# Zero products ahead of the first matmul, squares of the first tiles on POOL, and the first head's groups four dense steps later, in a two-block transformer kernel

## The chip, the cores and the metric

One core of one Trainium2 chip. The metric is the device time of one execution in microseconds (us). The kernel before takes 1307.53 us, the median of three runs (1307.06 to 1307.54).

## The reference

A sequence of 512 tokens with 1024 features passes two blocks. The first is gated DeltaNet (8 heads of 128, in chunks) and an MLP with a squared ReLU; the second has a short convolution, a stick-breaking attention, a spatial gate, an MLP and a gated projection. The change touches only the beginning of the first block:

```python
def rmsnorm(x, g):
    xf = x.astype(jnp.float32)
    y = xf * lax.rsqrt(jnp.mean(xf * xf, axis=-1, keepdims=True) + RMS_EPS)
    return (y * g.astype(jnp.float32)).astype(x.dtype)
...
    proj = h @ w_in
    qkv, gate, a_raw, b_raw = jnp.split(
        proj, [GDN_CONV_CH, GDN_CONV_CH + GDN_V, GDN_CONV_CH + GDN_V + GDN_HEADS], axis=-1)
    qkv = jax.nn.silu(causal_dwconv(qkv, conv_w)).astype(f32)
```

## The kernel before

The stream lies transposed in SBUF: `h` holds 8 tiles (`KT`) of 128 features by 512 tokens (`T`). Weights come in units of 128x1024 through two `raw` buffers. ACT rounds a unit to fp32r (`split_hi`, L398), DVE subtracts that from `raw` (`split_lo`, L405), and PE multiplies high and low parts in three products. The stream is split in the same way: ACT writes `xh` (L1736), DVE writes `xl` from `h` and `xh` (L2598). One **dense step** (`unit_steps`) is the three matmuls L429, L430 and L431 for one of a unit's 8 tiles; `unit_steps` is a generator, so PE's program can put other groups between dense steps.

The normalisation is applied late: the dense products run on the unnormalised stream, and `xrstd`, one factor for each token, multiplies their result. For it ACT squares the 8 tiles of `h` (L1739), DVE adds the squares (7 additions, L2610) into `accb`, PE sums over the partitions with a matrix of ones (`sums`, L773), and ACT takes a logarithm and an exponential (L1154, L1156). DVE then scales the decay inputs (L1770) and the first head's k (L1830, `dve_take_head`).

PE's order at the start is written out by hand in `pe_start`. `START_AT` says after how many dense steps each group comes: `mm` (decay inputs, L478), `sums`, `tr` (L485), `cum`, `row`, `k_first`, `spread`, then for head 0 `x(0)`, `tx(0)`, `k_second`, `x(1)`, `tx(1)`, `x(2)`, `tx(2)` and `q_first`. The `x` and `tx` groups are small products that invert a triangular matrix by doubling; between an `x` and its `tx` DVE masks the product (`dve_masks`, L1910, L1915), and after a `tx` it updates the inverse (`dve_updates`). After `START_STEPS` steps the period of head 1 begins (`pe_period`), whose groups (`x(0)` L578, `tx(0)` L627, `vtr`, `x(1)` L583, `tx(1)` L631, `x(2)` L588, `tx(2)` L636, `w` L681, ...) are followed each by the number of dense steps in `FIRST_FILL`. Periods 2 to 6 use `FILL`. The first 32 units always have 256 dense steps in all.

Head 2 needs its rows of decays spread over the partitions. ACT issues that transfer (`work<-rows`, L1183) behind the silu of head 0's v, then waits for it (L1205) before it scales the next k (L1254), for which DVE runs three taps (L1819) ahead of the mask of `tx(2)`.

POOL does nothing until the MLPs, where it adds squares (L1118, L1121) beside DVE.

Of the kernel before, what the change touches and what calls it, by code (L numbers as in the profile page):

```python
# [94 lines left out]
def build(nc, a, out):  # L95
    ctx = ExitStack()
    with ctx:
# [36 lines left out]
        def W(n, m=1):  # L134
            return work[:, n * T:(n + m) * T]
# [42 lines left out]
        def pc(name, n=0):  # L178
            lo = {"fn_g": NPAR, "q_g8": NPAR + KT}.get(name) or PC[name][0]
            return par[:, lo + n:lo + n + 1]  # L180

        def M(n, m=1):
            return more[:, n * T:(n + m) * T]
# [50 lines left out]
        out_d = sem("out_stored")  # L234
        zp = sem("zero_pad")
        tt0_d, id_d = sem("tt_pairs"), sem("tt_identity")
# [170 lines left out]
        def accumulator(u):  # L407


            if u.per == 0 and U_OUT1 + 2 <= u.const < U_OUT1 + 6:  # L410
                return ps[(0, 2, 1, 3)[u.const - U_OUT1 - 2]]
            return acc[u.const % 2]

        def unit_steps(pe, u, mh, ml, gate=None, order=range(KT), freed=None):

            b, (whi, wlo), dst = u.const % 2, slot(u), accumulator(u)
            pe.wait_ge(lo_done, u.number(1))
            if not u.known_below(2) and dst is acc[b]:  # L420


                beside = u.per == 0 and u.const in (U_OUT1 + 6, U_OUT1 + 7)
                pe.wait_ge(evac[b], u.half(-2 if beside else 0))
            for n, k in enumerate(order):
                if gate is not None:
                    gate(k)
                hi, lo = ch(whi, k), ch(wlo, k)
                nc.tensor.matmul(dst[:], hi, mh[:, k, :], start=(n == 0), stop=False)  # L429
                nc.tensor.matmul(dst[:], hi, ml[:, k, :], start=False, stop=False)  # L430
                mm = nc.tensor.matmul(dst[:], lo, mh[:, k, :], start=False, stop=(n == KT - 1))  # L431
                if n == KT - 1:
                    mm.then_inc(unit_done, 1)
                elif n == 1 and freed is not None:
                    mm.then_inc(freed, 1)
                yield
# [292 lines left out]
        FILL = [3, 3, 0, 3, 3, 3, 3, 2, 1, 2, 1, 2, 1, 2, 1, 2]  # L729
        FIRST_FILL = [3, 3, 0, 2, 3, 2, 3, 2, 1, 1, 1, 2, 1, 2, 2, 2]  # L730
        SHORT_FILL = [2, 2, 0, 2, 2, 2, 2, 2, 1, 2, 1, 1, 1, 1, 1, 2]
# [26 lines left out]

        def pe_start(pe, todo):
            def x_gate(k):  # L760
                pe.wait_ge(xl_done, k + 1)
# [8 lines left out]
            def sums():  # L770
                pe.wait_ge(s_keep, 16)
                pe.wait_ge(x_sq, KT - 1)
                nc.tensor.matmul(ps[0][:], ones, accb, start=True, stop=True).then_inc(rs_mm, 1)  # L773
# [28 lines left out]

        START_AT = [8, 10, 12, 15, 18, 20, 21, 29, 31, 33, 34, 36, 37, 39, 41]
        START_STEPS = 42
        assert sum(FILL) == START_STEPS - 5 * KT + sum(FIRST_FILL) == 4 * KT and sum(SHORT_FILL) == 3 * KT and sum(LAST_FILL) == 5 * (KT - 1)

# [305 lines left out]
        @block.gpsimd  # L1112
        def _(pool):
            for first in (2 * KT, 4 * KT):
                for m in range(6):
                    pool.wait_ge(sqs, first + m + 1)
                    if m == 0:
                        ins = nc.gpsimd.tensor_copy(accb, stream_sq[0])  # L1118
                    else:
                        pool.wait_ge(accs_t, first + m - KT)  # L1120
                        ins = nc.gpsimd.tensor_tensor(accb, accb, stream_sq[m % 2], ALU.add)  # L1121
                    ins.then_inc(accs_t, 1)
# [606 lines left out]
        def _(act):  # L1729
# [7 lines left out]
            split_hi(act, Unit(1))  # L1737
            for k in range(KT):
                nc.scalar.activation(W(11 + k), h[:, k, :], ACT.Square).then_inc(sqs, 1)  # L1739
            split_hi(act, Unit(2))  # L1740
# [82 lines left out]
        def dve_take_head(dve, sec, j):  # L1823
# [3 lines left out]
            if at > 0:  # L1827
                dve.wait_ge(conv_st, 3 * at)
                dve.wait_ge(tap3_d, at)
            nc.vector.tensor_tensor(xpad[:, 3:3 + T], acc[u.const % 2][:], xrstd, ALU.mult).then_inc(evac[u.const % 2], 1)  # L1830

# [164 lines left out]
        def dve_gdn(dve, i):  # L1996
# [22 lines left out]
            if i == 1:  # L2019
# [15 lines left out]
                for _ in dve_taps(dve, 2, 0):  # L2035
                    pass
                dve_gate(dve, 0)
                split_lo(dve, Unit(first))
# [6 lines left out]
            if b > 0:  # L2045
                dve_osum(dve, b)
            dve_masks(dve, i, 0, True, early)
            if i > 1:
                dve_gate(dve, b)
            dve_updates(dve, i, 0, True, early)  # L2050
# [540 lines left out]
        @block.vector  # L2591
        def _(dve):
            nc.vector.memset(xpad[:, 0:3], 0.0).then_inc(zp, 1)
            split_lo(dve, Unit(0))
# [10 lines left out]
            dve.wait_ge(s_keep, 16)  # L2605
            for k in range(1, KT):
                dve.wait_ge(sqs, k + 1)
                if k > 1:
                    dve.wait_ge(x_sq, k - 1)
                nc.vector.tensor_tensor(accb, W(11) if k == 1 else accb, W(11 + k), ALU.add).then_inc(x_sq, 1)  # L2610

# [3 lines left out]
            split_lo(dve, Unit(2))  # L2615
            dve.wait_ge(x_sq, KT - 1)
            nc.vector.memset(TT, 0.0)
# [129 lines left out]
```

## Time and profile before

| | |
|---|---|
| median of 3 runs | 1307.53 us |
| the profiled execution, its own time | 1307.65 us |
| its span, first to last instruction | 1305.9 us |
| outside the span | 1.75 us |
| PE busy | 1283.7 us (98%) |
| DVE busy | 957.8 us (73%) |
| ACT busy | 690.4 us (53%) |
| POOL busy | 16.5 us (1%) |

The busy time of PE is that of matmuls whose ends are modelled: dense matmuls follow each other at 0.23 us, and each is shown as 0.39 us long, so that an idle time printed behind one is 0.16 us short of the true gap.

### The profile page before, as it was taken

The numbers are of one execution on the slowest core, as the hardware profiler recorded it, in microseconds if no ns is written. First come the engines' busy times: TensorE is split into PE (matmuls) and PEld (weight loads), VectorE is DVE, ScalarE is ACT, GpSimd is POOL, SyncE is SP. The second block draws the span as 40 slices with busy tenths as digits, with TensorE's granted clock in tenths as the row PEclk, the third lists the DMA queues.
The fourth block names the chain that finished last, engine by engine and source line by source line (L and its number), as shares of the span: only waits on it lengthen the run. The fifth ranks groups of instructions, "written<-read, shape, count | busy, mean of one in ns | idle before, by whom it ended". The sixth has DMA issues, their size and how long they took to land.

```text
span 1305.9 us, 24372 instructions
## 1 busy us (share of the span) xinstructions
PE 1283.7 (98%) x9309; PEld 1085.8 (83%) x9309; DVE 957.8 (73%) x1543; ACT 690.4 (53%) x1100; POOL 16.5 (1%) x16
## 2 busy tenths in 40 slices
PE   6999999999999999999999999999999999999998
PEld 4788888888888998989887777788888989999876
DVE  7778778875767878777767777885777777776655
ACT  6766676765563434344446777733634444343452
POOL 0000000000000000000001000000000000000100
PEclk9999999999999999999999999999999999999999
DMA  4332222322234342333232222133243332322232
GB/s 162 79 92 63 77 77 69 81 66 82 72 107 132 96 125 91 105 96 98 65 98 81 65 65 71 59 97 113 83 159 97 98 96 96 98 96 88 75 95 97
DMA packets 40733, 119.52 MB, mean 92 GB/s; under 512 B 3984, under 2 KB 11600, under 8 KB 40656
## 3 DMA queue, kind: packets, MB, share of 16 engines
q1 hardware_dynamic: 33184, 114.78, 28.5%
q10 hardware_dynamic: 7472, 3.70, 1.7%
q8 instruction: 49, 0.80, 0.3%
q14 instruction: 28, 0.23, 0.1%
HBM read 116.34 MB, written 2.13 MB: 91 GB/s over the span
## 4 chain that ended last, share of the span: by engine, by line
PE 94%; DVE 3%; DMA 1%; ACT 1%; issue 1%; SPq 0%; ACTq 0%; DVEq 0%
PE acc L429 13%; PE acc L431 12%; PE acc L430 12%; PE ps L873 6%; PE ps L871 6%; PE ps L872 6%; PE acc L855 4%; PE acc L856 4%; PE acc L854 4%; PE ps L856 4%; PE ps L855 4%; PE ps L854 4%; PE ps L977 1%; PE ps L962 1%; PE ps L989 1%; DMA work<-rows 1%
## 5 line engine op out<-in xcount | busy, mean ns | idle before, releaser
L429 PE MATMUL acc<-xh,wh 128*128 128x512 f32 x624 | 259.2, 415 | 9.7 <-DVE xl L2598 8.8
L431 PE MATMUL acc<-xh,wl 128*128 128x512 f32 x624 | 244.6, 392 | 0.0
L430 PE MATMUL acc<-xl,wh 128*128 128x512 f32 x624 | 244.6, 392 | 0.0
L405 DVE TENSOR_TENSOR wl<-raw,wh 128x1024 fp32r<-128x1024 f32 x111 | 135.8, 1225 | 55.9 <-ACT wh L398 54.0
L429 PEld LDWEIGHTS acc<-xh,wh 128*128 128x128 f32 x624 | 117.9, 189 | 35.6 <-DVE wl L405 9.8
L431 PEld LDWEIGHTS acc<-xh,wl 128*128 128x128 f32 x624 | 117.6, 188 | 26.0
L430 PEld LDWEIGHTS acc<-xl,wh 128*128 128x128 f32 x624 | 118.0, 189 | 20.9 <-issue 1.2
L398 ACT ACTIVATE wh<-raw 128x1024 fp32r<-128x1024 f32 x111 | 115.8, 1049 | 29.7 <-DMA raw<-in_weights 20.3
L1495 ACT ACTIVATE wh<-raw 128x1024 fp32r<-128x1024 f32 x48 | 50.9, 1061 | 111.0 <-PE ps L856 111.0
L856 PE MATMUL acc<-yh,wl 128*128 128x512 f32 x256 | 99.9, 390 | 0.0
L855 PE MATMUL acc<-yl,wh 128*128 128x512 f32 x256 | 99.8, 390 | 0.0
L854 PE MATMUL acc<-yh,wh 128*128 128x512 f32 x256 | 99.8, 390 | 0.0
L856 PE MATMUL ps<-yh,wl 128*128 128x512 f32 x256 | 99.8, 390 | 0.0
L854 PE MATMUL ps<-yh,wh 128*128 128x512 f32 x256 | 99.6, 389 | 0.0
L855 PE MATMUL ps<-yl,wh 128*128 128x512 f32 x256 | 99.6, 389 | 0.0
L2184 DVE TENSOR_TENSOR h<-acc,h 128x512 f32<-128x512 f32 x56 | 38.4, 686 | 70.0 <-PE ps L856 70.0
L872 PE MATMUL ps<-xl,wh 128*128 128x256 f32 x288 | 81.5, 283 | 0.0
L873 PE MATMUL ps<-xh,wl 128*128 128x256 f32 x288 | 81.5, 283 | 0.0
L871 PE MATMUL ps<-xh,wh 128*128 128x256 f32 x288 | 81.4, 282 | 0.0
L1461 ACT ACTIVATE work<-work 128x512 f32<-128x512 f32 x64 | 40.5, 633 | 71.2 <-DVE work L2174 41.0
L1819 DVE SCALAR_TENSOR_TENSOR work<-xpad,par,work 128x512 f32<-128x512 f32 x72 | 53.6, 744 | 5.0 <-ACT work L1254 3.3
L1472 ACT ACTIVATE sums_hi<-work 128x1536 fp32r<-128x1536 f32 x24 | 35.8, 1491 | 39.6 <-DVE work L2239 39.6
(356 smaller groups left out, 2900.7 us busy)
## 6 DMA issues: line engine op xcount, KB each, us to landing
raw<-in_weights SPq DMA_DIRECT2D x208, 512.0 KB, 3.6
work<-rows ACTq DMA_DIRECT2D x14, 256.0 KB, 6.9
h<-in_xT SPq DMA_DIRECT2D x4, 512.0 KB, 6.6
outT<-h SPq DMA_DIRECT2D x8, 256.0 KB, 2.4
cst<-in_cst SPq DMA_DIRECT2D x1, 512.0 KB, 4.8
work<-in_pT SPq DMA_DIRECT2D x1, 512.0 KB, 4.6
kept<-in_keep SPq DMA_DIRECT2D x1, 208.0 KB, 6.2
work<-in_w_ab SPq DMA_DIRECT2D x1, 128.0 KB, 7.4
```

Of the source, the lines that this page charges most:

```text
L398: nc.scalar.activation(slot(u)[0][:], raw[u.const % 2][:], ACT.Copy).then_inc(hi_done, 1)
L405: nc.vector.tensor_tensor(lo[:], raw[u.const % 2][:], hi[:].bitcast(F32), ALU.subtract).then_inc(lo_done, 1)
L429: nc.tensor.matmul(dst[:], hi, mh[:, k, :], start=(n == 0), stop=False)
L430: nc.tensor.matmul(dst[:], hi, ml[:, k, :], start=False, stop=False)
L431: mm = nc.tensor.matmul(dst[:], lo, mh[:, k, :], start=False, stop=(n == KT - 1))
L854: nc.tensor.matmul(dst[:], hi, yh[:, y, :], start=(k == 0), stop=False)
L855: nc.tensor.matmul(dst[:], hi, yl[:, y, :], start=False, stop=False)
L856: mm = nc.tensor.matmul(dst[:], lo, yh[:, y, :], start=False, stop=(k == 3))
L871: nc.tensor.matmul(dst, ch(hi, k), mh(k), start=(k == 0), stop=False)
L872: nc.tensor.matmul(dst, ch(hi, k), ml(k), start=False, stop=False)
L873: mm = nc.tensor.matmul(dst, ch(lo, k), mh(k), start=False, stop=(k == 3))
L1819: nc.vector.scalar_tensor_tensor(out=buf, in0=xpad[:, t:t + T], scalar=cwall[:, sec * TAPS + t, j:j + 1], in1=buf, op0=ALU.mult, op1=ALU.a ...
```

## The change

It does five things.

1. DVE first clears `M(4)`, and PE multiplies these zeros five times into bank `ps[5]` ahead of its first dense step.
2. POOL squares tiles 0 to 3 of `h`, two tiles in one instruction, and adds the two results. ACT squares only tiles 4 to 7, two at a time. DVE has three additions left in place of seven: 1024, 1024 and 512 columns wide.
3. `sums` stands after 13 dense steps in place of 10, and each group from `tr` on after four more than before. `FIRST_FILL` has four steps fewer.
4. Unit 2 (head 0's q) accumulates in `ps[5]`, since `acc[0]` is not yet read when it begins; unit 4 waits for one evacuation fewer.
5. In the period of head 1 DVE's masks for `tx(0)` come ahead of the gate's evacuation and a `split_lo`.

```diff
         def accumulator(u):
...
+            if u.per == 0 and u.const == u_q(0).const:
+                return ps[5]
             return acc[u.const % 2]
...
-                pe.wait_ge(evac[b], u.half(-2 if beside else 0))
+                pe.wait_ge(evac[b], u.half(-2 if beside else -1 if u.per == 0 and u.const == 4 else 0))
...
-        FIRST_FILL = [3, 3, 0, 2, 3, 2, 3, 2, 1, 1, 1, 2, 1, 2, 2, 2]
+        FIRST_FILL = [2, 2, 0, 2, 2, 2, 2, 2, 1, 2, 1, 2, 1, 2, 1, 2]
...
         def pe_start(pe, todo):
+            pe.wait_ge(zp, 1)
+            for _ in range(5):
+                nc.tensor.matmul(ps[5][:], M(4)[:, 0:P], M(4), start=True, stop=True)
...
-        START_AT = [8, 10, 12, 15, 18, 20, 21, 29, 31, 33, 34, 36, 37, 39, 41]
-        START_STEPS = 42
+        START_AT = [8, 13, 16, 19, 22, 24, 25, 33, 35, 37, 38, 40, 41, 43, 45]
+        START_STEPS = 46
...
         @block.gpsimd
         def _(pool):
+            for n in range(2):
+                pool.wait_ge(s_x[n], 16)
+                nc.gpsimd.tensor_tensor(two_tiles(11 + 2 * n), h[:, 2 * n:2 * n + 2, :], h[:, 2 * n:2 * n + 2, :],
+                                        ALU.mult).then_inc(sq_pool, 1)
+            pool.wait_ge(sq_pool, 2)
+            nc.gpsimd.tensor_tensor(W(11, 2), W(11, 2), W(13, 2), ALU.add).then_inc(sq_pool, 1)
...
-            for k in range(KT):
-                nc.scalar.activation(W(11 + k), h[:, k, :], ACT.Square).then_inc(sqs, 1)
+            for n in range(2, 4):
+                nc.scalar.activation(two_tiles(11 + 2 * n), h[:, 2 * n:2 * n + 2, :], ACT.Square).then_inc(sqs, 4)
...
+                dve_masks(dve, 1, 0, True, True)
                 dve_gate(dve, 0)
                 split_lo(dve, Unit(first))
...
-            dve_masks(dve, i, 0, True, early)
             if i > 1:
+                dve_masks(dve, i, 0, True, early)
                 dve_gate(dve, b)
...
+            nc.vector.memset(M(4), 0.0).then_inc(zp, 1)
             nc.vector.memset(xpad[:, 0:3], 0.0).then_inc(zp, 1)
...
-            for k in range(1, KT):
-                dve.wait_ge(sqs, k + 1)
-                if k > 1:
-                    dve.wait_ge(x_sq, k - 1)
-                nc.vector.tensor_tensor(accb, W(11) if k == 1 else accb, W(11 + k), ALU.add).then_inc(x_sq, 1)
+            dve.wait_ge(sqs, 8)
+            nc.vector.tensor_tensor(W(15, 2), W(15, 2), W(17, 2), ALU.add).then_inc(x_sq, 1)
+            dve.wait_ge(sq_pool, 3)
+            dve.wait_ge(x_sq, 1)
+            nc.vector.tensor_tensor(W(11, 2), W(11, 2), W(15, 2), ALU.add).then_inc(x_sq, 1)
+            dve.wait_ge(x_sq, 2)
+            nc.vector.tensor_tensor(accb, W(11), W(12), ALU.add).then_inc(x_sq, 1)
```

POOL's program before, from its constants to the first MLP (`work<-work` are the additions of squares there):

```order
L2741 MEMSET const-uint8-127 128x1
L1112 UNCONDITIONAL_BRANCH
L1118 COPY work<-work 128x512
L1121 ISA
L1121 TENSOR_TENSOR work<-work 128x512 x5
```

and now, with the lines of the changed kernel:

```order
L2760 MEMSET const-uint8-127 128x1
L1121 UNCONDITIONAL_BRANCH
L1125 ISA
L1125 TENSOR_TENSOR work<-h 128x1024 x2
L1128 TENSOR_TENSOR work<-work 128x1024
L1133 COPY work<-work 128x512
```

Three POOL instructions of 1024 columns have come to the very start. Beside them runs this stretch of DVE's program, as it is now (`xl<-h,par,xh` is the low part of the stream, which dense steps 1 to 8 wait for tile by tile):

```order
L2609 MEMSET more 128x512
L2610 MEMSET xpad 128x3
L408 TENSOR_TENSOR wl<-raw,wh 128x1024
L2615 SCALAR_TENSOR_TENSOR xl<-h,par,xh 128x512 x8
L2619 TENSOR_TENSOR work<-work,par 128x256
L408 TENSOR_TENSOR wl<-raw,wh 128x1024
L2624 TENSOR_TENSOR work<-work 128x1024
L2627 TENSOR_TENSOR work<-work 128x1024
L2629 TENSOR_TENSOR work<-work 128x512
```

The order up to the second `split_lo` is the old one but for the first row; behind it three additions stand where seven stood.

DVE at the beginning of head 1's period before (`work<-ps,cst` are the masks, `wl<-raw,wh` is `split_lo`):

```order
L1819 SCALAR_TENSOR_TENSOR work<-xpad,par,work 128x512 x3
L1838 TENSOR_TENSOR work<-acc,work 128x512
L405 TENSOR_TENSOR wl<-raw,wh 128x1024
L1969 TENSOR_TENSOR work<-ps,work 128x512
L2003 COPY work<-work 128x4
L2007 TENSOR_TENSOR work<-work 128x4
L1910 TENSOR_TENSOR work<-ps,cst 128x64
L1915 TENSOR_TENSOR work<-ps,cst 128x64
L1925 TENSOR_TENSOR work<-ps,work 128x4x16
```

and now:

```order
L1834 SCALAR_TENSOR_TENSOR work<-xpad,par,work 128x512 x3
L1925 TENSOR_TENSOR work<-ps,cst 128x64
L1930 TENSOR_TENSOR work<-ps,cst 128x64
L1853 TENSOR_TENSOR work<-acc,work 128x512
L408 TENSOR_TENSOR wl<-raw,wh 128x1024
L1984 TENSOR_TENSOR work<-ps,work 128x512
L2018 COPY work<-work 128x4
L2022 TENSOR_TENSOR work<-work 128x4
L1940 TENSOR_TENSOR work<-ps,work 128x4x16
```

The two masks moved ahead of five other instructions; the updates of the inverse (last row) stay behind them.

## Rows read from the trace of the kernel before

**Rows 1.** The page: span, busy time, and the granted clock in 40 slices

```profile
span 1305.9 us, 24372 instructions
PE 1283.7 (98%) x9309; PEld 1085.8 (83%) x9309; DVE 957.8 (73%) x1543; ACT 690.4 (53%) x1100; POOL 16.5 (1%) x16
...
PEclk9999999999999999999999999999999999999999
```

**Rows 2.** Waits from 0 to 100 us: who for whom, us, times, longest

```profile
PE ps L627 <- DVE work L1915: 1.9, 1, 1.9
...
PE ps L636 <- DVE work L1915: 1.0, 1, 1.0
```

**Rows 3.** Timeline, 5 to 17 us: start, us, engine, line, names, [idle before]

```profile
6.53 1.23 DVE L405 TENSOR_TENSOR wl<-raw,wh 128x1024 fp32r<-128x1024 f32 x1 [5.65 <-ACT wh L398]
7.87 2.74 DVE L2598 SCALAR_TENSOR_TENSOR xl<-h,par,xh 128x512 fp32r<-128x512 f32 x4
8.76 0.76 PE L429 MATMUL acc<-xh,wh 128*128 128x512 f32 x1 [8.76 <-DVE xl L2598]
...
10.95 2.74 DVE L2598 SCALAR_TENSOR_TENSOR xl<-h,par,xh 128x512 fp32r<-128x512 f32 x4 [0.35 <-ACT xh L1736]
...
12.31 0.63 PE L431 MATMUL acc<-xh,wl 128*128 128x512 f32 x1
12.74 0.44 PE L429 MATMUL acc<-xh,wh 128*128 128x512 f32 x1
...
16.02 0.39 PE L431 MATMUL acc<-xh,wl 128*128 128x512 f32 x1
```

**Rows 4.** Timeline, 18 to 25 us: the additions' end, sums, tr

```profile
18.19 0.50 PE L429 MATMUL acc<-xh,wh 128*128 128x512 f32 x1
...
20.97 1.10 PE L773 MATMUL ps<-work,kept 128*128 128x512 f32 x2 [1.11 <-DVE work L2610]
...
22.14 0.39 PE L430 MATMUL acc<-xl,wh 128*128 128x512 f32 x1
...
24.15 1.06 PE L485 MATMUL ps<-kept,work 128*128 128x16 f32 x8 [0.69 <-DVE work L1770]
```

**Rows 5.** DVE's additions L2380: ns, least, median, most; first and last start

```profile
L2380 DVE TENSOR_TENSOR work<-work x7: 682/1369/1599, 675.9 to 700.9; 128x512 f32<-128x512 f32 x7
```

**Rows 6.** Timeline, POOL and DVE side by side in the two MLPs

```profile
675.31 1.29 POOL L1121 TENSOR_TENSOR work<-work 128x512 f32<-128x512 f32 x1 [0.43 <-ACT work L1518]
675.88 1.27 DVE L2380 TENSOR_TENSOR work<-work 128x512 f32<-128x512 f32 x1 [0.71 <-ACT work L1522]
...
1236.30 3.80 POOL L1121 TENSOR_TENSOR work<-work 128x512 f32<-128x512 f32 x2 [8.73 <-ACT work L1518]
1237.73 1.23 DVE L405 TENSOR_TENSOR wl<-raw,wh 128x1024 fp32r<-128x1024 f32 x1 [1.19 <-ACT wh L398]
1238.87 2.31 DVE L2358 TENSOR_TENSOR yl<-work,yh 128x1024 fp32r<-128x1024 f32 x1
...
1243.76 2.83 POOL L1121 TENSOR_TENSOR work<-work 128x512 f32<-128x512 f32 x2 [3.65 <-ACT work L1518]
1245.13 0.68 DVE L2361 TENSOR_TENSOR h<-ps,h 128x512 f32<-128x512 f32 x1
1246.00 1.14 DVE L2365 SCALAR_TENSOR_TENSOR xl<-h,par,xh 128x512 fp32r<-128x512 f32 x1 [0.20 <-ACT xh L1513]
```

**Rows 7.** Chain of waits, 52 to 75 us: start, us, what

```profile
58.83 8.39 DMA work<-rows
67.25 1.29 ACT work L1205 x4
...
69.95 0.72 ACT work L1254
...
72.26 0.75 DVE work L1819
...
73.20 0.64 PE ps L636 x16
```

More of the change, by code:

```diff
@@ L180, in pc, with two_tiles @@
             return par[:, lo + n:lo + n + 1]
+        def two_tiles(n):
+            return W(n, 2).rearrange("p (k t) -> p k t", k=2)
         def M(n, m=1):
@@ L234, in build @@
         out_d = sem("out_stored")
-        zp = sem("zero_pad")
+        zp, sq_pool = sem("zero_pad_then_zeros"), sem("first_squares_summed")
         tt0_d, id_d = sem("tt_pairs"), sem("tt_identity")
@@ L771, in sums @@
                 pe.wait_ge(s_keep, 16)
-                pe.wait_ge(x_sq, KT - 1)
+                pe.wait_ge(x_sq, 3)
                 nc.tensor.matmul(ps[0][:], ones, accb, start=True, stop=True).then_inc(rs_mm, 1)
@@ L1829, in dve_take_head @@
                 dve.wait_ge(tap3_d, at)
-            nc.vector.tensor_tensor(xpad[:, 3:3 + T], acc[u.const % 2][:], xrstd, ALU.mult).then_inc(evac[u.const % 2], 1)
+            nc.vector.tensor_tensor(xpad[:, 3:3 + T], accumulator(u)[:], xrstd, ALU.mult).then_inc(evac[u.const % 2], 1)
         def dve_gate(dve, j):
@@ L2615, in _ @@
             split_lo(dve, Unit(2))
-            dve.wait_ge(x_sq, KT - 1)
+            dve.wait_ge(x_sq, 3)
             nc.vector.memset(TT, 0.0)
```

## The prediction

> **What bounds the kernel now.** I read the page first, then the waits, then the timeline of the first 17 us and the chain of waits. The page shows PE busy for 1283.7 of 1305.9 us [rows 1]: PE is the bound, and only its gaps, or matmuls that run slowly, can be won back. PE's first work starts at 8.76 us, behind the first `xl` [rows 3]. The waits of the first 100 us name two later gaps [rows 2]: 1.9 and 1.0 us for masks in head 1's period (2.0 and 1.1 with the 0.16 us by which idle time is printed short). Two more stand at `sums` (1.11, truly 1.27) and at `tr` (0.69, truly 0.85) [rows 4]. The start also has slow matmuls: the first nine, from 8.76 to 12.74 us, take 0.43 us each, where those from 12.74 on to 16.02 take 0.23 [rows 3]. 512 columns at 0.43 us are TensorE's 1.2 GHz, at 0.23 about its 2.4 GHz. The engine had done nothing before 8.76.
>
> A difference below 0.2% (2.6 us) can't be told from none here.
>
> **The zeros.** DVE's memset is over soon after 1.3 us, so PE begins near 1.4. A float32 product of this size takes 0.94 us at the high clock (`sums` starts at 20.97, and the matmul behind it is through its slot 0.23 us before 22.14 [rows 4]); at half the clock 1.9 us. If the clock rises 4.0 us after the first product, as before (8.76 to 12.74 [rows 3]), two fit into the low stretch and three take 2.8 us: they end at about 8.1, before the old 8.76. If it doesn't rise they end near 10.8. The gain is at most nine times 0.2 us, 1.8 us, and only if nothing else holds unit 0 back.
>
> **What holds unit 0 back.** Step k needs tile k of `xl`. DVE makes the last tile at 10.95 + 2.74 = 13.69 us [rows 3]. PE follows a tile by 0.15 us (8.76 after 7.87 + 0.74) and a step takes 0.69, so unit 0 could end at 14.5 instead of 16.25. Every delay of `xl` now goes straight to PE.
>
> **POOL beside DVE.** This is the term that decides, and it can be read from the two MLPs [rows 6]. DVE's addition at 675.88 takes 1.27 us, where the shortest of the same line takes 0.68 [rows 5]: POOL's addition runs from 675.31 to 676.60, and DVE ends 0.55 us behind it. At 1246.00 an `xl` instruction of the very form of L2598 takes 1.14 us in place of 0.74 beside POOL's second addition. At 1237.73 the reverse is seen: DVE's 1.23 us come first, POOL's two additions need 3.80 us in place of 2.6, and DVE's next instruction (2.31 us, 1.1 too long) waits although it stood directly behind. `h<-ps` at 1245.13, with only one input in SBUF, loses nothing (0.68). So an instruction of DVE with two SBUF inputs and an addition on POOL exclude each other, each for its whole length, and when both have work they take turns.
>
> The Trainium skill says the same of the pair of ports that DVE and GpSimd share ("SBUF — State Buffer", Who interferes with whom): it is locked for a whole instruction, and the second to start is fully blocked. By its wording the earlier starter wins; these rows add that a waiting POOL instruction gets in between two adjacent ones of DVE.
>
> All eight `xl` and the `split_lo` ahead of them have two SBUF inputs. POOL's first square may start when tiles 0 and 1 are there (about 7.0 us, as ACT's `xh` does), finds `split_lo` running until 7.76 [rows 3], and comes next. Its length is not in the trace: twice the 1.29 us of 512 columns is 2.6 us; by DVE's ratio of 1.23 to 0.68 it is 2.3. I take 2.6, which scales POOL's own row rather than another engine's. "GPSIMD Engine Reference" of the Trainium skill (4.1, Engine selection) puts GpSimd at about twice VectorE's time for two inputs; by that it would be 2.45 us, and the sum 0.4 us less. No run shows it yet.
>
> - First square: 7.6 to 10.2; tile 0 of `xl` is ready at 10.8, not 8.6: 2.2 us.
> - Second square and the addition: each gets in between two tiles of `xl`, and costs its 2.6 us less about 0.2 us of overlap at the two handovers: 4.8 us.
> - Tiles 4 to 7 waited 0.35 us for ACT anyway: 0.4 us back.
>
> `xl` is thus complete at 13.7 + 6.6 = 20.3 us, and unit 0 ends at 21.1 in place of 16.25. The zeros win nothing then.
>
> **To `sums`.** `mm` and its surroundings take the same 1.95 us (16.25 to 18.19), and five dense steps 3.45 us: `sums` starts at 26.5. The squares are ready by then: `split_lo` 1.2, two additions of 1.2 and one of 0.7 behind 20.7 us give 25.2. Before it started at 20.97, so it is 5.5 us later. The old gap of 1.27 us is contained in this difference.
>
> **From `sums` to `tx(2)` of head 1.** `tr` comes 3.18 us after `sums` now, which is `sums` and then ACT and DVE; three dense steps of 0.69 in place of two fit into it, so the gap of 0.85 is filled and `tr` is no earlier. From there each group stands four steps later, at the same distances, and in the period of head 1 the chain is not PE's: a transfer of 8.39 us, ACT, three taps, then `tx(2)` at 73.20 [rows 7]. It starts behind head 0's v, which is tied to the groups. So `tx(2)` moves with `sums`, by 5.5 us. The moved masks let `tx(0)` go 2 us earlier, but this only shifts the gap: three dense steps fewer stand between `x(0)` and `tx(2)` (10 for 13), and the 2.0 and 1.1 us become some 5 us, all of them ahead of the same `tx(2)`. When `tx(2)` runs, 56 of the 256 steps are done instead of 55: 0.7 us won. Behind it the loops are unchanged; the fills there are 16 for 17 and I see no group that they make late. `ps[5]` for unit 2 and the lower evacuation count cost nothing: without them that unit would wait for L1830 behind `xrstd`.
>
> **Sum.** 5.5 - 0.7 = 4.8 us. Against the profiled execution's own time of 1307.65 that is 1312.4; it lies 0.1 above the median, so against the median **1312.3 us**, 0.37% slower. The case's own range is 1309.9 (one of POOL's three instructions costs nothing) to 1314.5.
>
> **Rivals.**
>
> *No blocking at this place (not slower).* POOL's instructions are different here (one tensor read twice), and its first work could come late. Then unit 0 ends at 14.5, `sums` is free at 14.5 + 1.95 + 3.45 = 19.9, and the squares are at hand about then: DVE's part, counted as above, would be over by 18.2, and ACT's two wide squares, done one after the other ahead of it, cost up to 1.5 us more. `sums` is 1.1 us earlier, plus 0.7: 1.8 us faster, **1305.7 us**. It decides where POOL delays the last `xl` by less than about 1.8 us in all. Against it stand three forms [rows 6].
>
> *The masks and the fills win more.* As the last one, and the transfer of head 2's rows lands sooner than 8.39 us after its issue, or `tx(2)` is reached another way. At most all gaps vanish: 1.27 + 0.85 + 2.0 + 1.1, and 1.8 for the slow matmuls, 7.0 us: 1300.5; half of the two mask gaps gives about **1304**. The chain [rows 7] speaks against it.
>
> *The clock falls again.* With blocking, PE runs one step in each of three stretches of about 3 us, and then waits on. If the clock goes back to 1.2 GHz, the next 4.0 us hold three steps in place of almost six: 2.0 us more, **1314.2 us**. For it: the engine was at the low level after idling until 8.76. Against: the page grants the full clock in every slice [rows 1], those with gaps of 1 to 2 us among them (though also in the first, where the matmuls are slow, so it is weak evidence). The Trainium skill ("TensorE: Matmul & The Clock Gate", Part 1) has an idle array return to the low clock; here it is not wholly idle.
>
> *The zeros don't raise the clock.* Without blocking this leaves unit 0 where it was, about 1307.5; with blocking it changes little, since five zeros at the low clock end near 10.8, as the first tile does.
>
> **Chances.** Blocking as forecast 0.55; with the clock falling 0.13; no or little blocking with some 1.8 us won or less 0.22; more won 0.10. Some of the first case's low end lies within 0.2% (up to 1310.1), 0.02. Faster by over 0.2% 0.10, within 0.2% 0.22, slower 0.68. The range, 1305.2 to 1314.5 us, takes in the first rival and nearly all of the clock's.
>
> **What would show it.** In the timeline after: POOL's three instructions between 7 and 16 us; L2615 with tiles 0, 1 and 2 about 3 us long each, the last `xl` near 20; PE with two gaps of some 2.5 us between its first three steps; `sums` near 26.5; `tx(2)` of head 1 near 78.7 with a wait of 3 us or more. If the last `xl` ends near 13.7 the forecast is wrong in its main term; if `tx(2)` does not follow `sums` by about 52 us, in its second.

## The result and the profile after

| | before | after |
|---|---|---|
| median of five runs, same chip | 1307.53 us (1307.06 to 1307.58) | 1317.65 us (1313.52 to 1318.90) |
| ratio, 95% interval | | 1.0068 (1.0058 to 1.0079) |
| profiled execution, its own time | 1307.65 us | 1317.65 us |
| its span | 1305.9 us | 1315.6 us |

The kernel became slower, as forecast, but by 10.1 us in the medians where 4.8 were forecast, and the time lies 3.2 us above the range. The runs after also lie 5.4 us apart, where those before lay within 0.5.

The page after, in the lines that answer to [rows 1], and the queue that brings PE's program:

```profile
span 1315.6 us, 24380 instructions
PE 1294.6 (98%) x9319; PEld 1091.2 (83%) x9319; DVE 961.9 (73%) x1540; ACT 688.1 (52%) x1094; POOL 24.1 (2%) x19
PEclk8999999999999999999999999999999999999999
q8 instruction: 49, 0.80, 0.3%
```

PE is busy 10.9 us longer. 6.7 us of that are the zeros, in a time in which it idled before; the other 4.2 us are old work that ran more slowly, which doesn't look like a loss on the page at all. The waits of PE from 0 to 125 us, to be held against [rows 2]:

```profile
PE acc L434 <- DVE xl L2615: 4.6, 3, 2.1
PE ps L641 <- DVE work L1930: 3.2, 1, 3.2
PE ps L636 <- issue: 1.2, 1, 1.2
PE acc L434 <- DVE wl L408: 1.0, 1, 1.0
```

The first is POOL's doing, the second is the gap ahead of `tx(2)` of head 1 (L641 now), which took over the two mask gaps. The third is new: PE stops for 1.2 us inside `tx(1)` of head 2 and waits for nothing that the profile knows. The timeline of DVE, POOL and PE at the start (against [rows 3]):

```profile
6.81 4.96 POOL L1125 TENSOR_TENSOR work<-h 128x1024 f32<-128x1024 f32 x2 [6.36 <-DMA h<-in_xT]
7.67 10.74 DVE L2615 SCALAR_TENSOR_TENSOR xl<-h,par,xh 128x512 fp32r<-128x512 f32 x8
10.17 0.47 PE L434 MATMUL acc<-xh,wh 128*128 128x512 f32 x1 [2.05 <-DVE xl L2615]
...
11.85 2.69 POOL L1128 TENSOR_TENSOR work<-work 128x1024 f32<-128x1024 f32 x1
...
12.38 0.67 PE L434 MATMUL acc<-xh,wh 128*128 128x512 f32 x1 [1.28 <-DVE xl L2615]
12.84 0.63 PE L435 MATMUL acc<-xl,wh 128*128 128x512 f32 x1
...
15.15 0.79 PE L434 MATMUL acc<-xh,wh 128*128 128x512 f32 x1 [1.25 <-DVE xl L2615]
...
21.10 0.39 PE L436 MATMUL acc<-xh,wl 128*128 128x512 f32 x1
```

Three instructions of POOL run between 6.8 and 14.5 us, the eight `xl` end at 18.4 in place of 13.7 us, and PE's first three steps stand 2.2 and 2.8 us apart. The step that begins at 12.38 has its matmuls 0.43 us apart again, although the zeros had raised the clock. The table by stretches shows that (start and end, length, busy time and count of PE, PEld, DVE, ACT, POOL, then the granted clock):

```profile
12.55:19.35 6.80, 5.55 (x13) 3.86 (x14) 6.80 (x8) 4.01 (x5) 2.00 (x1) 0.50 0.10 41
19.40:80.80 61.40, 55.88 (x750) 41.95 (x750) 45.58 (x110) 39.10 (x76) 0.00 (x0) 1.00 0.30 79
80.82:84.20 3.38, 3.38 (x13) 2.94 (x12) 3.28 (x8) 1.19 (x2) 0.00 (x0) 0.50 0.00 0
84.30:111.50 27.20, 25.82 (x351) 21.50 (x350) 19.31 (x47) 17.77 (x39) 0.00 (x0) 1.00 0.39 97
111.54:114.90 3.36, 3.36 (x9) 2.59 (x10) 3.18 (x8) 1.23 (x2) 0.00 (x0) 0.50 0.04 12
```

The granted clock is 0.50 three times, that is 1.2 GHz. A stretch of 3.4 us at half the clock holds 1.7 us less work, and PE counts as busy all through it, 3.38 of 3.38 us. The page's row of tenths has slices of 33 us and hides each of them. The kernel before has its clock at 1.00 all the way from 12.8 to 130 us. The two later stretches stand behind the two gaps:

```profile
75.74 0.39 PE L436 MATMUL acc<-xh,wl 128*128 128x512 f32 x1
79.34 0.64 PE L641 MATMUL ps<-work 64*32 64x64 f32 x16 [3.21 <-DVE work L1930]
...
109.12 0.31 PE L636 MATMUL ps<-work 32*32 32x32 f32 x6
110.67 0.25 PE L636 MATMUL ps<-work 32*32 32x32 f32 x5 [1.24 <-issue]
...
111.39 0.64 PE L550 MATMUL ps<-osh,ones_r 128*128 128x512 f32 x1
```

The account against [rows 7] and the span: `tx(2)` of head 1 at 79.34 in place of 73.20, 6.14 us; one step more done at that point, -0.69; the low stretch behind it, 1.70; the stop in head 2 at 1.24 in place of 0.26, 0.98; the low stretch behind it, 1.70. The sum is 9.8; the spans differ by 9.7.

### The profile page after: what moved, and what is told of

The parts are those of the page before. It is cut to its first block, busy times and chain, and to the rows that moved or that the text cites. A ratio compares the mean times of both kernels' runs of the same rounds, so it can differ in the third digit from the quotient of the medians.

```text
span 1315.6 us, 24380 instructions
## 1 busy us (share of the span) xinstructions
PE 1294.6 (98%) x9319; PEld 1091.2 (83%) x9319; DVE 961.9 (73%) x1540; ACT 688.1 (52%) x1094; POOL 24.1 (2%) x19
## 4 chain that ended last, share of the span: by engine, by line
PE 94%; DVE 3%; ACT 1%; DMA 1%; issue 1%; SPq 0%; ACTq 0%; DVEq 0%
PE acc L434 13%; PE acc L436 12%; PE acc L435 12%; PE ps L882 6%; PE ps L880 6%; PE ps L881 6%; PE acc L865 4%; PE acc L864 4%; PE acc L863 4%; PE ps L865 4%; PE ps L864 4%; PE ps L863 4%; PE ps L986 1%; PE ps L971 1%; PE ps L998 1%; PE ps L434 1%
```

## The experiments

The kernel before ran beside each: 1307.4 to 1307.8 us in the median. Eighteen kernels ran, on several chips, and each ratio is against the kernel before on the same chip, so kernels of different rows are best compared by their ratios.

| kernel | median us (range, runs) | ratio, 95% interval |
|---|---|---|
| e1, after without POOL's part | 1311.58 (1309.48 to 1313.08, 9) | 1.0028 (1.0018 to 1.0038) |
| e2, only POOL's part | 1313.34 (1310.82 to 1313.88, 5) | 1.0035 (1.0021 to 1.0049) |
| e3, only the zeros | 1308.92 (1306.94 to 1312.58, 9) | 1.0014 (1.0004 to 1.0024) |
| e4, only the masks | 1310.04 (1308.32 to 1310.63, 11) | 1.0018 (1.0009 to 1.0027) |
| e5, after, POOL behind `xl` | 1314.21 (1312.17 to 1315.46, 4) | 1.0047 (1.0032 to 1.0063) |
| e6, only the shift by four | 1308.80 (1308.02 to 1311.37, 11) | 1.0010 (1.0001 to 1.0019) |
| e7, before, fills late | 1309.30 (1308.58 to 1313.14, 10) | 1.0014 (1.0005 to 1.0024) |
| e8, masks, fills early | 1308.61 (1305.88 to 1310.94, 11) | 1.0002 (0.9993 to 1.0012) |
| e9, after, gap filled | 1315.12 (1313.16 to 1318.47, 5) | 1.0053 (1.0040 to 1.0067) |
| e10, e8, gap filled | 1307.42 (1306.27 to 1310.44, 11) | 0.9998 (0.9989 to 1.0007) |
| e11, after, fills early | 1315.20 (1313.21 to 1315.73, 5) | 1.0051 (1.0037 to 1.0065) |
| e12, e1, fills early, gap filled | 1310.70 (1309.25 to 1311.98, 11) | 1.0024 (1.0015 to 1.0033) |
| e13, before, 64 small products | 1326.80 (1326.53 to 1327.21, 4) | 1.0146 (1.0129 to 1.0163) |
| e14, before, one zero product | 1307.74 (1307.10 to 1308.47, 10) | 0.9996 (0.9987 to 1.0006) |
| e15, after, one zero product | 1316.16 (1313.37 to 1318.47, 4) | 1.0063 (1.0042 to 1.0085) |
| e16, after, 64 small products | 1331.57 (1330.23 to 1332.91, 4) | 1.0184 (1.0167 to 1.0201) |
| e17, after, fills late | 1319.69 (1317.18 to 1319.88, 5) | 1.0089 (1.0075 to 1.0102) |
| e18, masks, gap filled | 1307.71 (1307.13 to 1310.28, 11) | 1.0001 (0.9992 to 1.0010) |

### POOL's part: e1, e2, e5

e1 takes POOL's part out of the changed kernel; ACT squares all eight tiles, two at a time, and DVE adds four times.

```diff
-            for n in range(2):
-                pool.wait_ge(s_x[n], 16)
-                nc.gpsimd.tensor_tensor(two_tiles(11 + 2 * n), ...)
...
-            for n in range(2, 4):
+            for n in range(4):
                 nc.scalar.activation(two_tiles(11 + 2 * n), h[:, 2 * n:2 * n + 2, :], ACT.Square)
```

> The changed kernel with POOL idle: ACT squares all eight tiles, two at a time, and DVE makes four additions. Theory A (POOL and DVE take turns, and this moves the start): the last xl ends near 13.7 us instead of 18.4, unit 0 near 14.6 instead of 21.3, and sums near 21.7 (held by the squares) instead of 26.85. That is 5 us earlier; the time falls to 1308 to 1312, depending on whether the clock still falls in head 1's gap. Theory B (POOL is harmless, the moved groups and fills cost the time): within 1.5 us of the changed kernel's 1317.6.

e2 puts that part alone (part 2 of the change) into the kernel before.

> The kernel before with only the squares moved to POOL and widened. Theory A: the three xl tiles beside POOL take 2.3 to 2.9 us, the last xl ends near 18.4, sums starts near 23.2 instead of 20.97, tx(2) of head 1 comes 2.2 us later than 73.2; 1309.8 us if the granted clock stays up, up to 1314 if the gaps between the first steps let it fall. Theory B: 1306.5 to 1308, since DVE has fewer additions.

Without POOL the last `xl` ends at 13.14 us, `sums` starts at 20.86, `tx(2)` at 73.41, and the time is 6.1 us below the changed kernel's median. Alone, the part costs 5.9 us. So POOL's part is five to six tenths of the loss (by the ratios and by the medians), and it costs about the same with and without the rest. In e2 no zeros run, and `sums` starts at 25.6 us and not at 23.2: the clock rises only at 21.2, behind first steps that stand far apart. That was the first sign that the clock takes part.

e5 lets POOL wait until all of `xl` is written:

```diff
         def _(pool):
+            pool.wait_ge(xl_done, KT)
             for n in range(2):
```

> The changed kernel with one more wait: POOL's three instructions begin only when the last xl is done. Same work on POOL, not beside xl. Theory A: xl done near 13.7, POOL from 13.7 to 21 in turns with split_lo and the additions (DVE's instructions there grow from 1.2 to 3 us), squares ready near 22.5, sums near 22.5 against 26.85; 1312 to 1314. If POOL's work itself and not its place costs the time: 1317.

The timeline of DVE, POOL and PE there:

```profile
13.38 4.84 POOL L1126 TENSOR_TENSOR work<-h 128x1024 f32<-128x1024 f32 x2 [12.93 <-DVE xl L2616]
13.85 2.62 DVE L408 TENSOR_TENSOR wl<-raw,wh 128x1024 fp32r<-128x1024 f32 x1 [0.21 <-ACT wh L401]
16.39 2.91 DVE L2625 TENSOR_TENSOR work<-work 128x1024 f32<-128x1024 f32 x1
18.30 3.22 POOL L1129 TENSOR_TENSOR work<-work 128x1024 f32<-128x1024 f32 x1
21.56 1.23 DVE L2628 TENSOR_TENSOR work<-work 128x1024 f32<-128x1024 f32 x1 [2.25 <-POOL work L1129]
...
23.65 1.61 PE L782 MATMUL ps<-work,kept 128*128 128x512 f32 x2 [3.43 <-DVE work L2630]
```

`xl` is on time (13.3 us), but the lock has only moved on: `split_lo` takes 2.62 in place of 1.23 us, the addition 2.91 in place of 1.22, and `sums` waits 3.4 us, at its end for POOL's addition and the two of DVE behind it. The time, 1314.21, lies just above the band of theory A and 2.8 us below the rival's 1317. DVE's instruction with two inputs and POOL's exclude each other here too, and they take turns. How exactly they do can be read off by counting POOL's time from the end of the DVE instruction that was running when it started: `split_lo` ends at 16.47, POOL's second square at 18.22; the addition of DVE ends at 19.30, POOL's at 21.52. So counted, each of POOL's squares takes 1.75 us and its addition 2.2 us, here and in the profiles of the changed kernel, e2, e9, e11, e15 and e17. The longer times in POOL's rows (2.34 and 2.69 us) contain its wait for DVE. The Trainium skill ("SBUF — State Buffer", Who interferes with whom) calls the shared port pair an exclusive lock; the rows agree.

### One part at a time: e3, e4, e6, e7, e8

e3 is the kernel before with part 1 of the change, e4 with part 5, e6 with parts 3 and 4. e7 and e8 change the fills of head 1's period:

```diff
-        FIRST_FILL = [3, 3, 0, 2, 3, 2, 3, 2, 1, 1, 1, 2, 1, 2, 2, 2]
+        FIRST_FILL = [2, 2, 0, 2, 2, 2, 3, 3, 2, 2, 1, 2, 1, 2, 2, 2]
```

and, with the masks moved as well,

```diff
-        FIRST_FILL = [3, 3, 0, 2, 3, 2, 3, 2, 1, 1, 1, 2, 1, 2, 2, 2]
+        FIRST_FILL = [3, 3, 0, 3, 3, 4, 2, 2, 1, 1, 1, 2, 1, 1, 1, 2]
```

> The kernel before with only the five zero products. The first dense matmuls should be 0.23 us apart and unit 0 end near 14.5 instead of 16.25. But sums waits for the squares until 20.95 as before, so the 1.7 us won become gap: 1307.5 us, same as before within 0.5. If sums were not held by the squares, 1305.8.

> The kernel before with only the masks of head 1's tx(0) moved ahead. If tx(2) is set by the transfer of head 2's rows (theory A), tx(0) comes 2 us earlier, the 2.0 us gap in front of it goes, the gap in front of tx(2) grows from 1.1 to about 3 us, tx(2) stays at 73.2: 1307.5 us, up to 1309 if the larger gap lets the clock fall. If the gap at tx(0) was on the path (theory B): 1305.5.

> The kernel before with only START_AT, FIRST_FILL, the bank of unit 2 and its evacuation count changed. Theory A: sums near 21.6 (0.7 later, 3 more steps done), tx(2) of head 1 near 73.9 with a gap of some 3 us in front of it; 1307.5 us if the clock stays up, 1309 to 1311 if it falls behind that gap as it did in the changed kernel. Theory B (the shift is the loss): 1314 or more.

> The kernel before with three dense steps of head 1's period moved from ahead of tx(2) to behind it. Theory A: tx(2) stays at 73.2 and the gaps ahead of it grow by 2.1 us; the three steps come on top behind it: 1309.5 us, and 1.7 us more for each time the clock falls behind the longer gap. If PE sets tx(2): tx(2) at 71.1 and 1307.5.

> The kernel before with the masks moved, and three dense steps of head 1's period moved the other way, from behind tx(2) to ahead of it. Theory A: tx(2) stays at 73.2 with three more steps done and a gap of about 1 us: 1305.5 us if the 14 steps left behind tx(2) still cover the v and o groups, 1306.5 if one or two gaps of half a us open there. If PE sets tx(2): 1307.5 or more.

Alone, each part makes the kernel slower: POOL's by 5.9 us in the median, the zeros by 1.5, the masks by 2.5, the shift by 1.4. That is 11.3 us, not far from the 10.1 of all together. The intervals of the zeros and of the shift only just leave out a ratio of 1, so these two shares are uncertain. The zeros were expected to stay within 0.5 us of 1307.5 and came to 1308.92; e8 was expected to win 1 to 2 us and can't be told from the kernel before. `tx(2)` of head 1 stands at 72.95, 73.16, 73.85, 73.59 and 73.11 us: neither the masks nor the fills move it by more than 0.7 us, as the chain [rows 7] said. What they move is the gap. With the zeros, unit 0 runs at the high clock and 2.7 us of waiting appear ahead of `sums`; with the masks, 2.8 us ahead of `tx(2)`; with late fills, 2.6 us ahead of `tx(0)`. Behind the gap in the profiles of e4, e6, e7 and e8 the granted clock is 0.50 for 3.4 or 6.8 us, and so is it behind the stop in head 2 of e8:

```profile
75.10:78.40 3.30, 3.30 (x14) 3.08 (x13) 3.27 (x5) 0.85 (x2) 0.00 (x0) 0.50 0.14 19
78.60:105.80 27.20, 25.15 (x347) 20.95 (x346) 19.67 (x50) 18.25 (x41) 0.00 (x0) 1.00 0.32 95
105.85:109.20 3.35, 3.35 (x24) 2.16 (x22) 2.38 (x4) 0.57 (x1) 0.00 (x0) 0.50 0.02 5
```

The falls are not the same in each execution, and the kernel before is not safe from them. It has a gap of 1.9 us ahead of `tx(0)`; in its own profile and in e3's none follows it, in those of e13 and e14, with the same gap, the clock is 0.50 for 3.4 us behind it. Longer gaps have passed without a fall too: 2.7 us ahead of `sums` in e3, 2.6 us ahead of `tx(0)` in e6. The fastest runs of e8 (1305.88 to 1306.57) have a mean clock of 0.999 or 1.000, its slowest (1310.94) 0.997; the changed kernel's run from 0.998 at 1313.52 to 0.993 at 1318.90. One fall of 1.7 us is 0.0013 of the time, so 0.005 is about four of them, 6.5 us, where the runs differ by 5.4.

### Does the gap make the clock fall? e9, e10, e18

Products of the stream in dense size, 0.23 us each, go into a bank that is idle, ahead of head 1's `tx(2)`: 13 in the changed kernel (e9), 5 in e8 (e10), 11 in e4 (e18).

```diff
         def tx_group(pe, i, r, late, early):
...
+            if isinstance(i, int) and i == 1 and r == 2:
+                pe.wait_ge(qkd_d, 1)
+                for _ in range(13):
+                    nc.tensor.matmul(ps[5][:], xh[:, 0, 0:P], xh[:, 0, :], start=True, stop=True)
```

> The changed kernel, with 13 dense-sized products (512 columns, 0.23 us each, 3.0 us in all) of the stream into the idle bank ps[5] ahead of tx(2) of head 1, where PE otherwise idles 3.4 us. Theory (the clock falls because of that gap, 1.7 us a fall): the low stretch behind 79.3 us goes, tx(2) stays at 79.3 within 0.3 us, and the time falls by 1.5 to 2 us to about 1316, with less spread between runs; if the later fall in head 2 was a consequence as well, by 3.4 to about 1314. Rival (the fall has nothing to do with the gap): a low stretch remains at 80 to 84 us and the time stays at 1317.6. Second rival (the chain feeding tx(2) is slowed by the products): tx(2) comes later than 79.6 and the time rises.

> The kernel before with the masks moved, FIRST_FILL = [3, 3, 0, 3, 3, 4, 2, 2, 1, 1, 1, 2, 1, 1, 1, 2] and 5 dense-sized products (1.15 us) in the remaining 1.4 us gap ahead of head 1's tx(2). Its twin without the products took 1308.6 with runs from 1305.9 to 1310.9. Theory (the spread is the clock falling behind this gap or not): the low stretch at 75 us goes and the median comes near the fast end, 1306.3 to 1307.2, with a range below 3 us. Rival (falls come from elsewhere, as in head 2): the median stays at 1308 to 1309 with the same spread.

> The kernel before with the masks moved and its own fills, and 11 dense-sized products (2.5 us) in the gap of 3.0 us ahead of head 1's tx(2). Its twin without the products took 1310.0 (1308.3 to 1310.6) with one low stretch behind tx(2) and no long stop in head 2. Theory (the fall behind tx(2) is all that the moved masks cost; the stop needs fewer than 17 steps behind tx(2)): tx(2) at 73.2, no low stretch behind it, no stop over 0.3 us, and 1306.8 to 1308.3, equal to the kernel before. Rival: a stop and a low stretch appear in head 2 because the products shift PE's program, and the time is 1308.5 to 1310.

e9 by stretches:

```profile
20.20:79.30 59.10, 56.66 (x710) 42.49 (x709) 43.90 (x107) 37.55 (x74) 0.00 (x0) 1.00 0.28 82
79.40:84.00 4.60, 4.60 (x69) 4.04 (x70) 3.42 (x7) 3.52 (x6) 0.00 (x0) 1.00 0.00 0
84.00:108.80 24.80, 22.72 (x292) 18.87 (x290) 18.78 (x45) 16.15 (x36) 0.00 (x0) 1.00 0.33 92
108.90:115.70 6.80, 6.57 (x61) 4.91 (x62) 3.97 (x9) 2.12 (x4) 0.00 (x0) 0.50 0.14 55
```

`tx(2)` stays at 79.40, and behind it the clock is now 1.00. The median falls by 2.5 us against the changed kernel's, though the two intervals overlap; the profile is the slowest of e9's five runs. The fall in head 2 stays, so it was no consequence of the first. In e10 the stretch at 75 us has gone as well, and in head 2 one of 6.8 us remains behind a stop of 2.2 us. e18 came to 1307.71, 2.3 us below its twin e4, with nine of eleven runs between 1307.1 and 1308.2; its profile is one of the two others (1310.28) and still has 3.4 us of low clock, behind a gap of 1.7 us that the 11 products did not fill: `tx(2)` stood at 74.36 there, because the transfer of the rows took 9.60 us in place of 8.28 in e4, and had landed before the products began. The three pairs with and without products differ by 2.5, 1.2 and 2.3 us in the same direction. By their intervals only e4 and e18, which ran on the same chip, hardly overlap; the clock of the single runs says more. Its mean is 0.999 or 1.000 in 2 of e4's 11 runs and in all 11 of e18's, in 4 of e8's 11 and in 10 of e10's 11. So a gap makes a fall likely, and work that computes nothing of use holds the clock. It makes it likely and no more, since a single execution can go either way. No version beats the kernel before; the best, e10 and e18, equal it.

### The gap filled by dense steps: e11, e12, e17

```diff
-        FIRST_FILL = [2, 2, 0, 2, 2, 2, 2, 2, 1, 2, 1, 2, 1, 2, 1, 2]
+        FIRST_FILL = [2, 2, 0, 3, 3, 3, 2, 1, 1, 1, 1, 1, 2, 1, 1, 2]
```

is e11; e12 is e1 with these fills and 5 products in the rest of the gap; e17 goes the other way:

```diff
-        FIRST_FILL = [2, 2, 0, 2, 2, 2, 2, 2, 1, 2, 1, 2, 1, 2, 1, 2]
+        FIRST_FILL = [1, 1, 0, 2, 2, 1, 3, 3, 2, 2, 1, 2, 1, 2, 1, 2]
```

> The changed kernel with FIRST_FILL = [2, 2, 0, 3, 3, 3, 2, 1, 1, 1, 1, 1, 2, 1, 1, 2]: 13 dense steps ahead of head 1's tx(2) as before the change, in place of 10, and three fewer behind it. Theory (tx(2) is tied to the rows transfer, so the gap only has to be filled): tx(2) stays at 79.3, its gap shrinks from 3.4 to about 1.3 us, 2.1 us are won, and 1.7 more where the clock no longer falls behind it: 1313.8 to 1315.5. Rival (the steps push tx(2) later): tx(2) at 81, and the time stays within 0.7 of 1317.6, since the three steps are then missing behind it as gaps of groups in the second half of the head.

> The changed kernel without POOL's part (all squares on ACT, two tiles at a time), with the fills of the run before, and 5 dense-sized products of the stream (1.15 us) in what is left of the gap ahead of head 1's tx(2). The candidate for a version that keeps the useful parts. Theory: tx(2) at about 73.4 as without POOL; its gap of 3.4 us is filled by two more dense steps, the products hold the clock, so 1311.6 - 2.1 - 1.7 = 1307.8, equal to the kernel before; below 1306.5 only if the fall in head 2 goes too. Rival (something later sets the time, such as the issue gap in the first pass of the loop or the groups behind tx(2) that lost three steps): 1309.5 to 1311.5.

> The changed kernel with FIRST_FILL = [1, 1, 0, 2, 2, 1, 3, 3, 2, 2, 1, 2, 1, 2, 1, 2]: 7 dense steps ahead of head 1's tx(2), 19 behind it (before the change 13 and 17, now 10 and 16). Over 18 profiles the stop of PE in head 2 was under 0.3 us with 17 or 20 steps behind tx(2), 1.0 to 1.5 us with 16 (2.4 where 13 products had been put in), and 2.1 to 2.8 with 13 or 14. Theory (that count sets the stop): no stop over 0.3 us in head 2 and so no low clock there; tx(2) stays at 79.3 with its gap 2.1 us longer, in all 5.4, and the clock falls behind it. Two steps of 0.69 each stand behind where a stop of 1.2 and a fall of 1.7 were: 1.4 us lost against the 1.2 and sometimes 1.7 us, so 1315.5 to 1317.5, about the time of the changed kernel. Rival (the four later steps at the start, not the fills, make the stop): it stays at 1.0 us or more, and the time is 1318.5 to 1320.

e11 wins 2.4 us: its gap is 1.9 us (`tx(2)` at 79.91), no low clock follows it in the profile, but the stop in head 2 is 2.3 us and a fall comes behind that. e12 has no fall at `tx(2)` either, has the longest stop (2.8 us), and its time is within the rival's band, 2.9 us above the theory's. Both give part of the win back in head 2. In e17 the stop stays at 1.7 us with 19 steps behind `tx(2)`, so the theory that their number sets it has fallen; its time of 1319.69 is the rival's. e17's profile happens to tell something else. There the clock did not fall at the start:

```profile
12.55:19.35 6.80, 4.98 (x24) 3.40 (x26) 6.80 (x8) 4.04 (x5) 1.59 (x1) 1.00 0.11 44
19.40:74.50 55.10, 50.12 (x682) 37.45 (x674) 42.57 (x105) 35.36 (x71) 0.00 (x0) 1.00 0.31 88
74.60:81.30 6.70, 4.45 (x55) 3.67 (x56) 3.17 (x8) 4.11 (x6) 0.00 (x0) 0.50 0.01 2
```

and PE's `sums` starts at 24.53, with the last `xl` at 18.0, where the changed kernel's starts at 26.85 with the last `xl` at 18.4. The same program, as far as that point, differs by 2.3 us, of which 0.4 come from `xl` and 1.9 from the clock.

### The stop in head 2: e13 to e16

e13 and e16 begin with 64 products of 16 columns, in the kernel before and in place of the five zeros of the changed one; e14 and e15 begin with one product of 512 columns.

```diff
         def pe_start(pe, todo):
+            pe.wait_ge(zp, 1)
+            for _ in range(64):
+                nc.tensor.matmul(ps[5][:, 0:16], M(4)[:, 0:P], M(4)[:, 0:16], start=True, stop=True)
```

> The kernel before, with 64 products of zeros of 16 columns ahead of the first dense step, where PE idles anyway. Ten profiles so far have PE's longest unexplained stop in head 2 right behind its matmul record number 1094 (three behind 1097), whatever line stands there. Theory (PE waits for the next part of its own program, at a fixed count of instructions): the stop moves to an earlier place of the program, by as many instructions as were put in, near 98 us, and stands again behind about record 1094. Rival (it belongs to a place in the program or to the first pass of the loop): it stays between L631 and L644 near 102 us. Where it is long (over 1 us), a low clock of 3.4 or 6.8 us follows it; time 1307.5 to 1309.

> The kernel before with one 512-column product of zeros ahead (0.9 or 1.9 us of work, over long before 8.7 us). It changes no order and no gap, and so serves as a second look at the kernel before. Theory (length of the stop in head 2 is chance): its stop in head 2 has any length from 0 to 2.8 us, 1307.5 within 0.8 us in the median. Rival (it follows from the order of the program): 0.3 us or less, as in the profile of the kernel before.

> The changed kernel with one product of zeros in place of five. Since POOL holds the stream back until 10 us and later, the zeros should be worth nothing here: same time as the changed kernel, 1315 to 1318, and the dense steps start at 10.2, 12.4 and 15.2 us as with five. If the five zeros are worth something, it is the clock of the first steps: then about 1 us slower. Its stop in head 2 tells by its length whether that is chance: about 1.2 us if it goes with the program, 0 to 2.8 if it is chance.

> The changed kernel with 64 products of zeros of 16 columns in place of the five of 512. Theory (program part at a fixed count): the stop of head 2 comes behind record 1094 again, earlier in the program than L636 of head 2's tx(1), about 104 us, and is 1 to 3 us long; behind it and behind tx(2) of head 1 the clock falls, 1.7 us for each stretch of 3.4 us. Rival: the stop stays at 109 us. Time 1315 to 1318.

e13 and e16 miss their times by far, by an error in my choice of filler: small float32 products are not cheap.

```profile
1.46 27.49 PE L762 MATMUL ps<-more 128*128 128x16 f32 x128 [1.46 <-DVE xpad L2598]
```

64 of them take 27.3 us, 0.43 us each, so all of the kernel starts 20 us late, and the times only say that. Their profiles still answer for the stop. It did not stay behind record 1094 of the matmuls: e16's stands behind record 1222, 10 records further on in the program than the changed kernel's, and is 1.0 us; e13's is 0.13 us, behind record 1222 too, in the old place of the program. In the form in which it was put, the theory of a fixed count has fallen. But count all records of PE, its matmuls, its weight loads and those of its sequencer. Then 2241 or 2242 stand ahead of this point in the other 18 profiles (e9's stop behind matmul 1097 among them), and 2497 and 2498 in e16 and e13. That is 256 more, and 64 small products are just 128 matmul and 128 weight load records. So the count is fixed after all, give or take whole pieces of 256 records: what was put in had the length of one such piece. If such a piece is one 16 KB packet of the queue of instructions, q8, a record is 64 bytes, an estimate from these two numbers.

What the stop waits for shows in another view, that of DMA traffic, here the changed kernel from 108.3 to 109.5 us and e7, which has no such stop, from 102.5 to 103.7 us:

```profile
q8 instruction: 1, 0.02, 4.8%
```

One packet of 16 KB of instructions is on the way in each. It starts at 108.45 us in the changed kernel and the stopped matmul runs at 110.68, 2.23 us behind. The same is found in all 18 other profiles of kernels here: the record on which PE stops, or reaches the same point without a long stop, starts 2.2 to 2.45 us behind the start of a packet on this queue (e13's at 121.72, 2.26 us behind). What differs is the work that PE still has in hand when the packet starts. In e7, seven dense matmuls and the sixteen small ones of `tx(1)` cover it:

```profile
102.81 0.40 PE L431 MATMUL acc<-xh,wl 128*128 128x512 f32 x1
...
104.19 0.39 PE L431 MATMUL acc<-xh,wl 128*128 128x512 f32 x1
104.51 0.44 PE L631 MATMUL ps<-work 32*32 32x32 f32 x16
```

In the changed kernel only about two dense matmuls and six small ones do, the last of them at 109.2. In e10, e11 and e12 PE has nothing in hand, and stops for 2.2, 2.3 and 2.8 us. So the stop is PE waiting for its own program, in the first pass of the loop. That is read from the times in all 20 profiles and from the count; no run took the transfer away. What decides how far ahead of need the packet is asked for stays open. The length is not chance, as I had expected for e14: the profiles of e2, e3, e4, e7, e13, e14 and e18 have stops of at most 0.3 us, as the kernel before has, and the changed kernel, its near twin e15 and e5 have 1.24, 1.27 and 1.42. Neither the shift alone decides (e8 has none and stops for 2.1 us) nor the number of steps behind `tx(2)` (e17).

## Why the prediction was right in direction and wrong in size

In short, the steps that failed are two that the sum put at nothing, and one that it sized wrongly. The clock was taken to stay up behind the first steps and behind the gap ahead of `tx(2)`; it fell three times, 5.3 us. The loops were taken to run unchanged; PE stopped 1.0 us longer in their first pass. And POOL's delay of the stream was put at 5.5 us and measured 4.0.

**The zeros** ended at 8.1 us as forecast and won nothing: with one in place of five (e15) the median is 1316.16, inside the spread of the changed kernel. They did raise the clock, at 5.7 us, but in the changed kernel's profile it fell again at 12.55 and rose at 19.4, where it first rises in e15's.

**POOL beside DVE** is shown in direction and mechanism: all three instructions get in between tiles of `xl`, and without them (e1) the last tile is back at 13.1 us. The size was wrong. I took 2.6 us for each of POOL's instructions of 1024 columns; counted from DVE's release, its squares take 1.75 us and its addition 2.2. The 2.34 us of the second square's row look like the 2.3 that the prediction named and set aside, but 0.6 of them are waiting. The first three tiles were forecast to lose 2.2, 2.4 and 2.4 us, and lost 1.4, 1.6 and 2.1; 0.4 came back at the fifth, as forecast. The last `xl` is 4.7 us late and not 6.6.

**The time to `sums`** looks like a hit (26.85 against 26.5), but two errors cancel. With the clock held (e17, its `xl` set 0.4 us later) `sums` would start at 24.9, 4.0 us later than before: POOL's term was 1.5 us too large. The falling clock, 6.8 us at 0.50 between 12.55 and 19.35, which cost 1.9 us against e17, was missing. The third rival named exactly this and priced it at 2.0 us; it had got 0.13.

**From `sums` to `tx(2)`** the distance was forecast as unchanged, and it is: 52.2 us before, 52.5 after, 52.3 in e17, whatever masks and fills do. The chain was read rightly.

**"0.7 us won", since one step more is done at `tx(2)`,** did not last. The matmul with which PE goes on behind the stop in head 2 starts at 110.68, where the one at which it paused before (ten matmuls further in the program, 0.1 us) started at 102.80: 7.9 us later, about the 6.1 and the 1.7 of the low stretch alone. The stop grew by 1.0 and took the 0.7. **"Behind it the loops are unchanged"** failed: the loop's instructions are, but not the moment at which they are in the core.

**The gap ahead of `tx(2)`** was forecast at some 5 us, or 3 and more; it is 3.4, and 1.2 and 1.0 us more stand ahead of it, at 66.19 (for `split_lo`) and ahead of `x(2)` at 73.52. That it "only shifts" failed: in this profile the gap is followed by a fall of the clock, 1.7 us, which is gone in e9, where the gap is filled. I had asked the question of the clock for the start alone. The argument against it, full clock in every slice of the page [rows 1], was weak as the text said, and it was weak for all of the kernel: slices of 33 us can't show a stretch of 3.4. A second fall, 1.7 us, comes behind the stop.

The terms as measured: 4.0 us from POOL's delay of `xl` (forecast 5.5), 1.9 from the clock at the start (none), 0.2 between `sums` and `tx(2)` (none), 1.7 from the fall behind it (none), 1.0 from the stop less 0.7 for the step (forecast -0.7 alone), 1.7 from the fall behind the stop (none): 9.8 us where 4.8 were forecast.

The first rival (no blocking) and the fourth (zeros that don't raise the clock) are excluded by the timeline; the second (masks and fills win) by e4, e7 and e8.

## What to carry to other kernels

Of a gap that "only moves", ask what stands behind it: one gap of 3 us in place of two of 1 and 2 us cost here, in the profiled execution, a stretch at half clock as well, in which PE shows as fully busy, so look at the granted clock by stretches of a few us and not by the page's slices. POOL is no free helper beside DVE instructions with two inputs in SBUF; moving its work 6 us later only changed which of them it held up. A row of POOL's that ran beside DVE contains its waits: count from DVE's release. A forecast that hits an intermediate time has not confirmed its terms: check each term against its own row.

## What was not expected of the hardware

- PE can stop for its own program in a loop's first pass: 1.0 to 2.8 us in twelve profiles, always at the same count of PE's records, or 256 further where 256 had been put in; PE goes on 2.2 to 2.45 us behind the start of a 16 KB packet of instructions.
- The clock fell behind gaps in one execution and not in another of the same instructions: e17 and the changed kernel differ at the start, where their programs are the same, by 1.9 us. The Trainium skill ("TensorE: Matmul & The Clock Gate", HAM oscillation — how this bites in real kernels) has the clock fall where matmuls come in short groups with waits between them; the stretches above agree, but here dense work stood around single gaps of 1.2 to 3.8 us, and gaps of 1.9 us (e11) and 2.7 us (e3) passed without a fall.
- A float32 product of 16 columns took 0.43 us at the low clock (e13), as long as one dense matmul of 512 columns there. And 27.5 us of them without a pause did not raise the clock: the dense matmuls behind them were still 0.43 us apart, until 32.6, where five zero products of 512 columns had raised it by 5.7.
